# Turning half of x and the cross attention's keys by square transposes and transfers, in a hybrid layer kernel of 256 tokens

## What is computed

```
h2 = rms_norm(x, norm_mlp_g)                                   # first layer, end
x = x + square(relu(h2 @ w_mlp_up)) @ w_mlp_down               # blocks "up", "down"

hn = rmsnorm(x, g_mix);  proj = hn @ w_in_2                    # second layer, "in2"
...                                                            # retention, fox attention
h = x + concat([ret, fox]) @ w_out_2                           # "out2"

def memory_cross_attention(hn, mem, ...):                      # hn = rmsnorm(h, g_xattn)
    q = rmsnorm((hn @ w_xq).reshape(B, T, 4, 256), g_xq)       # "xq"
    k, v = split(rmsnorm(mem, g_mem) @ w_xkv)                  # "kv"
    k = rmsnorm(k.reshape(B, M, 4, 256), g_xk)
    p = softmax(einsum('bthd,bmhd->bhtm', q, k) * 256 ** -0.5)
    return einsum('bhtm,bmhd->bthd', p, v) @ w_xo              # "xo"
```

## Time and profile before

| | us |
|---|---|
| median of three runs | 880.29 |
| lowest, highest | 879.72, 880.34 |
| the profiled execution, its own time | 880.51 |
| its span in the trace | 878.7 |
| TensorE busy in it | 871.6 |
| VectorE, ScalarE, GpSimd busy | 599.9, 439.2, 183.3 |

### The profile page before, as it was taken

One profiled execution on the slowest core, in us unless ns is written; L12 is line 12 of the kernel. 1 busy time (PEld: TensorE's weight loads), 2 busy tenths in 40 slices (PEclk: granted clock), 3 DMA queues, 4 the chain that ended last, 5 costly groups with the idle time before them and its releaser, 6 DMA issues.

```text
span 878.7 us, 12721 instructions
## 1 busy us (share of the span) xinstructions
PE 871.6 (99%) x5023; PEld 750.3 (85%) x5023; DVE 599.9 (68%) x875; ACT 439.2 (50%) x613; POOL 183.3 (21%) x214
## 2 busy tenths in 40 slices
PE   9999999999999999999999999999999999999998
PEld 6897888888888999988888889888888888888886
DVE  5478988998796566745456848877786576665742
ACT  6265456864555555533345436546554544443530
POOL 0432234863110000000003322100100024444500
PEclk9999999999999999999999999999999999999999
DMA  8774542445146556555667965524442567775862
GB/s 299 199 260 145 186 150 88 130 131 166 48 145 197 190 189 191 191 192 192 191 192 224 281 143 193 191 96 139 160 134 94 159 199 219 218 220 154 255 218 72
DMA packets 87651, 154.67 MB, mean 176 GB/s; under 512 B 10528, under 2 KB 18512, under 8 KB 87472
## 3 DMA queue, kind: packets, MB, share of 16 engines
q1 hardware_dynamic: 80352, 144.55, 50.9%
q0 software_dynamic: 4720, 5.86, 3.6%
q10 hardware_dynamic: 2528, 3.56, 1.2%
HBM read 147.53 MB, written 1.44 MB: 170 GB/s over the span
## 4 chain that ended last, share of the span: by engine, by line
PE 98%; ACT 1%; DVE 0%; issue 0%; ACTq 0%
PE gemm L540 74%; PE gemm L1049 5%; PE mixbank L1049 5%; PE mixbank L603 1%; PE mixbank L702 1%; PE mixbank L727 1%; PE mixbank L808 1%; PE mixbank L1214 1%; PE gemm L1242 1%; PE mixbank L713 1%; PE mixbank L750 1%; PE mixbank L902 0%; PE gemm L614 0%; ACT w_hi L1304 0%; PE mixbank L1132 0%; PE mixbank L1192 0%
## 5 line engine op out<-in xcount | busy, mean ns | idle before, releaser
L1874 DVE TENSOR_TENSOR w_lo<-raw,w_hi 128x2048 fp32r<-128x2048 f32 (+3 forms) x132 | 287.8, 2187 | 180.2 <-ACT w_hi L1304 180.0
L1304 ACT ACTIVATE w_hi<-raw 128x2048 fp32r<-128x2048 f32 (+3 forms) x140 | 255.4, 1833 | 201.8 <-DMA raw<-in_w_in_dram 53.2
L540 PE MATMUL gemm<-w_hi,s_hi 128*128 128x512 f32 (+3 forms) x784 | 207.7, 385 | 0.6 <-ACT s_hi L1340 0.3
L540 PE MATMUL gemm<-w_hi,s_lo 128*128 128x512 f32 (+3 forms) x784 | 201.6, 377 | 0.0
L540 PE MATMUL gemm<-w_lo,s_hi 128*128 128x512 f32 (+3 forms) x784 | 201.6, 377 | 0.0
L540 PEld LDWEIGHTS gemm<-w_hi,s_lo 128*128 128x128 f32 x784 | 142.7, 188 | 27.6
L540 PEld LDWEIGHTS gemm<-w_lo,s_hi 128*128 128x128 f32 x784 | 142.6, 188 | 27.4
L540 PEld LDWEIGHTS gemm<-w_hi,s_hi 128*128 128x128 f32 x784 | 139.9, 188 | 26.0 <-issue 1.8
L2745 POOL TENSOR_TENSOR sm<-sm 128x2 f32<-128x2 f32 (+5 forms) x13 | 21.6, 1663 | 400.1 <-DVE sm L1935 296.1
L373 POOL DMA_DIRECT2D hid_moved<-hid_blocks x96 | 54.7, 578 | 72.9 <-DVE hid_blocks L2687 70.7
L2739 POOL TENSOR_TENSOR w_lo<-raw,w_hi 128x2048 fp32r<-128x2048 f32 x8 | 36.8, 4620 | 36.1 <-ACT w_hi L1304 36.1
(11 more groups left out here) (365 smaller groups left out, 1181.9 us busy)
## 6 DMA issues: line engine op xcount, KB each, us to landing
raw<-in_w_in_dram SPq DMA_DIRECT2D x40, 1024.0 KB, 5.3
raw<-in_w_mlp_up_dram SPq DMA_DIRECT2D x16, 1024.0 KB, 5.7
raw<-in_w_mlp_down_dram SPq DMA_DIRECT2D x16, 1024.0 KB, 5.1
raw<-in_w_gate_dram SPq DMA_DIRECT2D x10, 1024.0 KB, 5.5
raw<-in_w_up_dram SPq DMA_DIRECT2D x10, 1024.0 KB, 5.1
raw<-in_w_down_dram SPq DMA_DIRECT2D x10, 1024.0 KB, 5.6
raw<-in_w_out_dram SPq DMA_DIRECT2D x8, 1024.0 KB, 5.1
raw<-in_w_xkv_dram SPq DMA_DIRECT2D x8, 1024.0 KB, 5.1
```

Of the source, the lines that this page charges most:

```text
L540: return nc.tensor.matmul(G[b % 2][t][:, 0:width], lhs, rhs, start=kt == 0 and not (low_x or low_w), stop=kt == blk["kt"] - 1 and (low_x i ...
L1304: nc.scalar.activation(w_hi[:, n % SLOTS, 0:kn, 0:width], raw[:, n % SLOTS, 0:kn, 0:width], ACT.Copy)\
L1874: V.tensor_tensor(w_lo[:, s, 0:kn, 0:width], raw[:, s, 0:kn, 0:width], w_hi[:, s, 0:kn, 0:width].bitcast(F32), ALU.subtract)\
```

## The change

It has four parts.

1. **Half of x after "down".** The columns 0 to 511 of x, complete after `B_DN`, are turned by two square transposes on VectorE and 16 transfers issued by GpSimd, into the two halves of the free tile `hid`, while `B_DN + 1` runs. ScalarE and VectorE make `s_hi` and `s_lo` of row tiles 0 to 3 from there, ahead of the end of that block. TensorE turns only the second half of x, after the first quarter of `B_2`.
2. **The keys' norm.** ScalarE's squares move from behind "out2"'s first block into the fox attention (after the exponentials of k = 3), VectorE's sum into its step k = 6. The scaling moves from behind the turn of x to just ahead of the reading of `B_O2`'s result, and is done by eight operations of 256 columns.
3. **The keys' turn.** Four square transposes on VectorE while `B_O2 + 1` runs, then 16 transfers: eight issued by GpSimd, eight by ScalarE ahead of the turn of x for "xq". The 16 transposes on TensorE and their four copies are gone; the products read the moved keys.
4. **The corners.** ScalarE's split of the second chunk of `B_GA + 1` moves behind the four corner copies.

The core of the diff:

```diff
-            turn(xtile, lambda q: [("ev0", B_DN + 1 + q // 2), ("ev1", B_DN + 1 + q // 2), ("hid_lo", 16)])
-            for j in range(4):
-                mm(B_2 + j, turned=None if j else 16)
+            mm(B_2, turned=16, quarters=[0])
+            turn(xtile, lambda q: [("ev0", B_DN + 2), ("ev1", B_DN + 2), ("hid_lo", 16)], banks=range(2, 4))
+            mm(B_2, turned=16, quarters=[1, 2, 3])
+            for j in range(1, 4):
+                mm(B_2 + j)
...
             mm(B_XQ, turned=28)
-            pe.wait_ge(sem("x_k"), 1)
-            cross_operands(range(4))
             def cross_logits(k):
-                pe.wait_ge(sem("xT_act"), 3 if k < 2 else 4)
-                pe.wait_ge(sem("xT_dve"), 3 if k < 2 else 4)
+                pe.wait_ge(sem("x_moved"), 16 * 8)
+                pe.wait_ge(sem("ret_w_and_keys_in"), 16 + 16 * 8)
+                pe.wait_ge(sem("xT_act"), 1 if k < 2 else 2)
+                pe.wait_ge(sem("xT_dve"), 1 if k < 2 else 2)
...                                                            # ScalarE
-            split(B_GA + 1, 1)
             for u in range(4):
                 act.wait_ge(sem("inv_p"), 6 + u + 1)
                 nc.scalar.activation(PS[64:128, 4 * u:4 * u + 4, 0:64], ...)
+            split(B_GA + 1, 1)
...
             begin(B_DN + 1)
-            turn_hi(NORMS["mix2"])
+            moved_hi(x2_part(1), "x2_moved", "mix2", range(2))
+            turn_hi(NORMS["mix2"], banks=range(2, 4))
...
             for k in attention(WORK_A, ...):
+                if k == 3:
+                    act.wait_ge(sem("ev0"), B_KV + 2)
+                    act.wait_ge(sem("ev1"), B_KV + 2)
+                    act.wait_ge(sem("foxT_pe"), 8)
+                    nc.scalar.activation(SQX, KV[:, :, 0:D], ACT.Square).then_inc(sem("x_sqk"), 1)
...
             begin(B_O2)
-            act.wait_ge(sem("ev0"), B_O2)
-            act.wait_ge(sem("ev1"), B_O2)
-            nc.scalar.activation(SQX, KV[:, :, 0:D], ACT.Square).then_inc(sem("x_sqk"), 1)
             begin(B_O2 + 1)
+            act.wait_ge(sem("squares_turned"), 4)
+            move(act, X_MOVED, X_BLOCKS, "ret_w_and_keys_in", range(2, 4))
             turn_hi(NORMS["xattn"])
...
-            cross_operand(0)
-            cross_operand(2)
             query_sums(0)
             cross_operand(4)
...                                                            # VectorE
                 begin(B_DN + j)
+                if j == 1:
+                    moved_lo(x2_part(1), "mix2", range(2))
...
+                if j == 0:
+                    for t in range(NT):
+                        ins = V.transpose(x2_part(0)[:, NCOL * t:NCOL * t + NCOL], x[:, t, 0:NCOL])
+                    ins.then_inc(sem("squares_turned"), 1)
-            turn_lo(NORMS["mix2"])
+            turn_lo(NORMS["mix2"], banks=range(2, 4))
...
                 if k == 6:
                     turn_lo(banks=range(2))
+                    dve.wait_ge(sem("x_sqk"), 1)
+                    link(V.tensor_reduce(SSX, SQX...))
+                    V.tensor_scalar(SSX, ...).then_inc(sem("root_asked"), 1)
...
             begin(B_O2)
-            dve.wait_ge(sem("x_sqk"), 1)
-            link(V.tensor_reduce(SSX, ...))
-            V.tensor_scalar(SSX, ...).then_inc(sem("root_asked"), 1)
+            link(V.tensor_tensor(vec[:, V_XK:V_XK + 256], vec[:, V_XK:V_XK + 256], vec[:, V_XQ:V_XQ + 256], ALU.mult))
+            dve.wait_ge(sem("root"), root("xk"))
+            for t in range(NT):
+                for h in range(4):
+                    k = KV[:, t, 256 * h:256 * h + 256]
+                    ins = V.scalar_tensor_tensor(k, k, RNX[:, 4 * t + h:...], vec[:, V_XK:V_XK + 256], ALU.mult, ALU.mult)
+            link(ins)
             residual(B_O2, 0)
-            begin(B_O2 + 1)
+            turn_squares(X_BLOCKS, KV).then_inc(sem("squares_turned"), 1)
+            split(B_XQ, 0)
+            split(B_XQ, 1)
             residual(B_O2 + 1, 1)
...                                                            # the four operations of L2570 and L2573 go,
...                                                            # and cross_operand(1) and (3); then GpSimd
             norm_power(1)
+            pool.wait_ge(sem("squares_turned"), 2)
+            move(pool, x2_part(1), x2_part(0), "x2_moved")
             norm_power(2)
...
             power("xk", RNX[:, 0:8], SSX, 8)
+            pool.wait_ge(sem("squares_turned"), 4)
+            move(pool, X_MOVED, X_BLOCKS, "x_moved", range(2))
             norm_power(4)
```

More of the change, by code:

```diff
@@ L377, in moved, with x2_part @@
             return v.rearrange("p (t k n) -> p k t n", t=NT, n=P)[:, kt]
+        def x2_part(n):
+            return hid[:, n].rearrange("p f n -> p (f n)")
         def token_tile(v):
@@ L1213, in cross_logits @@
                     for e in range(2):
-                        last = nc.tensor.matmul(M[k % 2][:, SEQ * j:SEQ * j + SEQ], xqT[:, 2 * h + e, P * t:P * t + P], xkT[:, 2 * h + e, :],
-                                                start=e == 0, stop=e == 1)
+                        o = M[k % 2][:, SEQ * j:SEQ * j + SEQ].rearrange("p (t n) -> p t n", n=P)
+                        last = nc.tensor.matmul(o, xqT[:, 2 * h + e, P * t:P * t + P], moved(X_MOVED, 2 * h + e), start=e == 0, stop=e == 1)
                 last.then_inc(sem("att_logits"), 1)
@@ L1321, in project, with moved_hi @@
                 nc.scalar.activation(dst, G[b % 2][0][:, 0:blocks[b]["n"]], ACT.Copy, scale=scale).then_inc(sem("ev0"), 1)
-            def memory_hi(pairs):
-                for q in pairs:
-                    act.wait_ge(sem("mem_moved"), 16 * 16)
-                    for kt in (2 * q, 2 * q + 1):
-                        ins = nc.scalar.activation(token_tile(s_hi[:, kt, :]), moved(MEM, kt), ACT.Copy, scale=gains[:, NORMS["mem"], kt:kt + 1])
-                    sig(ins, "turn_hi")
+            def moved_hi(v, name, norm, pairs):
+                for q in pairs:
+                    act.wait_ge(sem(name), 16 * 16)
+                    for kt in (2 * q, 2 * q + 1):
+                        ins = nc.scalar.activation(token_tile(s_hi[:, kt, :]), moved(v, kt), ACT.Copy, scale=gains[:, NORMS[norm], kt:kt + 1])
+                    sig(ins, "turn_hi")
+            def memory_hi(pairs):
+                moved_hi(MEM, "mem_moved", "mem", pairs)
             def turned_by_pe():
-                return seen.get("turn_hi", 0) + 1 - (KT // 2 if seen.get("turn_hi", 0) >= 20 else 0)
+                n = seen.get("turn_hi", 0)
+                return n + 1 - (2 if n >= 14 else 0) - (KT // 2 if n >= 20 else 0)
             def turn_hi(norm=None, banks=range(4)):
@@ L1913, in turn_lo, with moved_lo @@
                     sig(ins, "turn_lo")
-            def memory_lo(pairs):
+            def moved_lo(v, norm, pairs):
                 for q in pairs:
@@ L1919, in memory_lo @@
                     for kt in (2 * q, 2 * q + 1):
-                        ins = V.scalar_tensor_tensor(token_tile(s_lo[:, kt, :]), moved(MEM, kt), gains[:, NORMS["mem"], kt:kt + 1],
+                        ins = V.scalar_tensor_tensor(token_tile(s_lo[:, kt, :]), moved(v, kt), gains[:, NORMS[norm], kt:kt + 1],
                                                      token_tile(s_hi[:, kt, :]).bitcast(F32), ALU.mult, ALU.subtract)
                     sig(ins, "turn_lo")
+            def memory_lo(pairs):
+                moved_lo(MEM, "mem", pairs)
             def turn_squares(dst, src):
@@ L2564, in _ @@
             mean_squares(4)
-            link(V.tensor_tensor(vec[:, V_XK:V_XK + 256], vec[:, V_XK:V_XK + 256], vec[:, V_XQ:V_XQ + 256], ALU.mult))
-            dve.wait_ge(sem("root"), root("xk"))
-            kv = [KV[:, t, 0:D].rearrange("p (h d) -> p h d", d=256) for t in range(NT)]
-            for t in range(NT):
-                ins = V.tensor_tensor(kv[t], kv[t], spread(RNX[:, 4 * t:4 * t + 4], 2, 256), ALU.mult)
-            link(ins)
-            for t in range(NT):
-                ins = V.tensor_tensor(kv[t], kv[t], spread(vec[:, V_XK:V_XK + 256], 1, 4), ALU.mult)
-            ins.then_inc(sem("x_k"), 1)
             dve.wait_ge(sem("root"), root("xattn"))
```

43 lines of the change are left out of this document (20 added, 23 removed).

## The result

The changed kernel takes 885.38 us (median of 4 runs, 884.76 to 885.67) against 880.32 us (879.72 to 880.44) of the kernel before on the same chip: a ratio of 1.0058, with an interval of 1.0046 to 1.0070. Forecast were 877.0 us and a range of 876.2 to 878.6. The prediction was wrong in its sign: the kernel is 5.1 us slower and not 3.3 us faster. Its profiled execution took 884.76 us, with a span of 882.6 us.

The account below looks back on a forecast made before the run. TensorE, busy 871.6 of 878.7 us, was taken as the bound. Terms -1.75 - 1.06 + 0.1 - 0.55 = -3.26 us took 880.51 to 877.25, or 877.0 for the median; range 876.2 to 878.6.

Parts of the forecast that it names:

- the transfers of the keys: Ahead of the turn for "xq": ScalarE's eight issues at 0.45 us end at 627.0, before its high parts; cost 0.
- Rival (b): Before "xq": ScalarE's eight issues are slow and TensorE waits; at 1.3 us each 882.4 us; chance 0.04.
- The keys' turn on TensorE: Before the first logits: the keys' 16 transposes leave TensorE's chain and nothing replaces them, -1.75 us.
- rival (a): At the first logits or "out2": TensorE stands still about as long as the transposes took; 878.8 us, chance 0.12.
- rival (c): On TensorE: the 24 removed transposes each cost their full 0.272 us, 6.5 us in all; 873.1 us, chance 0.02.
- VectorE around "out2": At "out2": VectorE's scalings, square transposes and splits just fit the tightest cover; 0, up to +0.5 us.
- Half of x: Between "down" and "in2": eight transposes fewer and no wait for the reading, -1.06 us; second "in2" block stalls, +0.1.
- The corners: At the corner copies: TensorE's wait goes once ScalarE's split moves behind them, -0.55 us, between -0.3 and -0.61.
- The keys' norm: In the fox attention: squares and sum fit where ScalarE and VectorE stood idle, cost 0.
- The bounds of the sum: For the whole kernel: the terms at their bounds give 876.4 to 879.4 us.

Follow-up runs that it names:

- the kernel with ScalarE's transfers alone: Changed kernel with weight loads of the second "xq" block and GpSimd's eight transfers held back until ScalarE's eight landed: 884.74 us, one run.
- part 1 alone: Kernel before with only half of x after "down" turned by square transposes and GpSimd's transfers: 879.70 us, ratio 0.9995.
- the last experiment: Changed kernel with all 16 transfers issued by GpSimd and ScalarE's squares of the memory behind its splits of the second "in2" block: 877.60 us, ratio 0.9974.
- the four surroundings: ScalarE's eight issues with or without GpSimd's transfers and weight loads: 5.50 us with neither, 6.12 loads only, 8.38 GpSimd only, 10.51 both.

## Why the prediction was wrong, point by point

**The step that failed** is the one on the transfers of the keys: "At 0.45 us they end at 627.0, at 0.65 at 628.6 [...] I take 0.45: 0". The eight issues took 10.51 us, 1.31 each. There are two mistakes in it. First, I chose between two rows, ScalarE's 0.31 to 0.47 us and GpSimd's 0.65, by the engine; ScalarE's row was of another transfer, and the floor for this one proved to be 0.65 us on either engine. By itself that would have cost little: in the kernel with ScalarE's transfers alone the eight ended at 626.40, ScalarE began its high parts at 626.45, and from the start of TensorE's turn to the first product of "xq" it took 2.03 us instead of 1.81. The issues also began at 620.86 and not at the 623.4 that I had put down. The cover itself was sized rightly: 10.51 us of issues made the first product 5.2 us late, which leaves 5.3 us of cover against my 5.0. Second, and this made the loss, I took an issue's duration for a constant of the instruction. The rows of before hold no issue of ScalarE with other transfers in flight, so they couldn't bound it from above; I used their two ends as if they could. Rival (b) named this mechanism, and with 0.04 was given too small a chance. The Trainium skill ("DMA: Bandwidth & Descriptors", Issuing engines are not separate DMA queues) says that transfers of all issuing engines run on the same 16 DMA engines and interleave, and that several issuers save only the time to initiate them. The trace agrees on the first: the load of weights that SyncE issued at 625.55 beside the keys' transfers took 9.2 us to land, and 5.3 us for the same chunk before. The saving came out negative: GpSimd alone issued all 16 in 10.31 us and delayed nobody, and the split over two issuers cost 7.5 us.

**The price in rival (b)** came out at 877.0 + 8 x 1.31 - 5.0 = 882.5 us; measured were 885.4. Missing in the formula is the clock. From the first product of "xq" to the first logits it was 17.34 us with all transfers on GpSimd (628.09 to 645.43) and 19.47 in the changed kernel: 2.1 us for a clock that fell while TensorE stood still. The other 0.8 us are about the distance (0.9) of the kernel with GpSimd alone from the forecast.

**The keys' turn on TensorE, -1.75**: right. The 17.34 us stand against 19.11 of before, -1.77. The queries' chain needed nothing of it as cover; rival (a) didn't happen, and rival (c) neither.

**VectorE around "out2", 0**: nearly right. The scalings took 3.26 us (forecast 3.2), the square transposes 2.48 (2.4). TensorE's turn of x for "xq" lasts 1.96 us from its start to the first product with all transfers on GpSimd, instead of 1.81, so +0.15, in my bounds.

```profile
613.85 3.26 DVE L2583 SCALAR_TENSOR_TENSOR mix<-mix,sm,vec 128x256 f32<-128x256 f32 x8
618.35 2.48 DVE L1941 STREAM_TRANSPOSE mix<-mix 128x512 f32<-128x512 f32 x4
```

**Half of x, -1.06 and +0.1**: the mechanism was right, the stall was mis-sized. After, the eight transposes take 0.79 us of TensorE, and the stall at the second block is the 0.37 us of the experiment with part 1 alone (466.28 to 468.46 is 2.18 us for eight products that take 1.81 without it):

```profile
456.33 1.03 PE L608 MATMUL mixbank<-cst,x 128*128 128x128 f32 x8
457.12 1.17 PE L545 MATMUL gemm<-w_hi,s_hi 128*128 128x512 f32 x4
...
466.28 1.07 PE L545 MATMUL gemm<-w_hi,s_lo 128*128 128x512 f32 x4
467.43 1.20 PE L545 MATMUL gemm<-w_lo,s_hi 128*128 128x512 f32 x4
468.46 1.07 PE L545 MATMUL gemm<-w_hi,s_hi 128*128 128x512 f32 x4
```

That makes -1.14 + 0.37 = -0.77 us instead of -0.96; the medians of part 1 alone show -0.52, within their noise. That ScalarE's late squares cause the stall is shown by the last experiment, where moving the memory's squares took it away.

**The corners, -0.55**: right, -0.61 in the trace; -0.44 in the medians, within their noise. **The keys' norm, 0**: right; 880.17 against 880.31, and no new wait. **The bounds of the sum**: the lower end of 876.4 doesn't follow from the terms; -1.75, -1.06 and -0.61 from 880.29 make 876.9.

**What is left over.** The terms as the traces show them, without ScalarE's issues, sum to -1.77 + 0.15 - 0.77 - 0.61 = -3.0 us. The kernel with all transfers on GpSimd gained 2.5 in the medians and 2.7 in the spans. Its trace shows where the rest went, at the turn of the second half of x:

```profile
455.57 1.40 DVE L2445 SCALAR_TENSOR_TENSOR x<-gemm,sm,x 128x512 f32<-128x512 f32 x2
455.72 1.07 PE L545 MATMUL gemm<-w_hi,s_lo 128*128 128x512 f32 x4
457.07 1.06 PE L608 MATMUL mixbank<-cst,x 128*128 128x128 f32 x8 [0.29 <-issue]
```

The turn follows the four products at 1.35 us instead of 0.91, so 0.44 us are lost. It needs VectorE's reading of "down"'s last block, which ended at 456.97; in the changed kernel, where the chunk that VectorE splits ahead of it had come 1.5 us sooner, the reading began at 454.07 and nothing was lost. The forecast left 0.6 us of cover there (the reading done at 457.0, TensorE asking at 457.6) and gave the place no price; here TensorE asks at 456.63, 0.3 us ahead of the reading's end. The changed kernel's trace has luck of its own beside that: the first product of its first block comes at 7.26 us instead of the 7.71 of the other two traces, a place that the change doesn't touch. So at the turn of x for "xq" it is 1.8 us ahead of before, and the kernel with GpSimd alone 1.0.

**What stays open.** That ScalarE's issue is held while transfers of other queues are in flight is shown by the four surroundings. Whether that traffic holds the issue itself, or only makes ScalarE's own pieces land later (6.1 to 9.8 us after their issue in the changed kernel, 2.1 to 2.5 us alone) so that more of them pile up, no run separates. The 7.62 us with half of the pieces fit both. Against the second, in the kernel with all 16 on ScalarE the seventh issue was at the floor with six of its own still in flight, and in the changed kernel the fifth took 1.92 us with four. Why GpSimd's issue isn't held, and what exactly is full when ScalarE stands, no run shows either.

## To carry to other kernels

An issue of a transfer on a computing engine is a piece of that engine's list whose length depends on what else is in flight: read it from a row with the same form and the same traffic, and where there is none, bound it from above by more than the longest quiet row, or put the issue on an engine that has nothing waiting behind it. Before a critical engine's neighbour is given such work, multiply its worst price by the count and hold that against the cover; here 8 x 0.63 us was all the cover. And where a forecast has TensorE standing still for some microseconds, add the price of the clock behind it to the wait itself.

## What the runs showed of the hardware

**An issue on ScalarE** of a transfer of 64 KB from 32 to 32 partitions in 128-byte pieces took 0.64 to 0.65 us at least, with 512 pieces as with 256 (0.625), and up to 2.07 us beside other transfers. GpSimd's issues of the keys took 0.65 to 0.70 us in every kernel, whatever was in flight.

**The two kinds of queue move the same bytes differently.** The queues of the changed kernel from 619 to 642 us, with packets, MB and share of 16 engines:

```profile
q10 hardware_dynamic: 4224, 0.52, 21.5%
q0 software_dynamic: 256, 0.52, 15.3%
```

q10 carries ScalarE's eight transfers and q0 GpSimd's: 4224 packets against 256 for the same 0.52 MB, and 1.4 times the DMA engines' time.

**TensorE's clock** fell to 1.2 GHz in the changed kernel while TensorE stood idle for 4.83 us between two full stretches, and the stretch behind lost 2.1 us by it; with the loads held back, it fell after a wait of 2.7 us too. With ScalarE's issues behind its squares it fell after the wait of 1.9 us, when TensorE had been at work again for a microsecond. In the kernel whose GpSimd waits for ScalarE, with waits of 1.8 and 1.5 us, it stayed at full speed in the profiled execution (two of its eight runs have a mean clock of 0.998). So the length of one wait doesn't tell the two apart. The stretches, first the kernel with the late issues, then this one:

```profile
642.00:645.00 3.00, 3.00 (x9) 2.01 (x7) 3.00 (x2) 1.20 (x2) 0.00 (x0) 0.53 0.53 194
...
640.00:645.00 5.00, 3.28 (x12) 2.10 (x12) 3.60 (x2) 3.68 (x3) 0.00 (x0) 1.00 0.81 249
```
